# Four layer norms whose squares are taken during the product ahead of them, about a mean of four chunks, and summed on VectorE

## What is computed

```python
x_lat = layer_norm_2(DEEPNORM_ALPHA * x_lat + (1 + g1) * m_lat, ln1_g[l], ln1_b[l])      # ln1_l
f_lat = swiglu(x_lat * (1 + sc2) + sh2, w_ffn_gate[l], w_ffn_up[l], w_ffn_down[l])
x_lat = layer_norm_2(DEEPNORM_ALPHA * x_lat + (1 + g2) * f_lat, ln2_g[l], ln2_b[l])      # ln2_l

def layer_norm_2(x, g, b):
    mu = jnp.mean(xf, axis=-1, keepdims=True)
    var = jnp.mean(jnp.square(xf - mu), axis=-1, keepdims=True)
    y = (xf - mu) * lax.rsqrt(var + NORM_EPS) * g + b
```

## Time and profile before

| | |
|---|---|
| time, median of 3 runs | 2913.59 us (2911.48 to 2914.23) |
| the profiled execution: its own time, its span | 2915.59 us, 2913.8 us |
| TensorE busy (matmul) | 2683.3 us, 92% of the span |
| VectorE busy | 788.1 us, 27% |
| ScalarE busy | 457.9 us, 16% |
| mean granted TensorE clock | 0.965 |

### The profile page before, as it was taken

One profiled execution on the slowest core, in us unless ns is written; L12 is line 12 of the kernel. 1 busy time (PEld: TensorE's weight loads), 2 busy tenths in 40 slices (PEclk: granted clock), 3 DMA queues, 4 the chain that ended last, 5 costly groups with the idle time before them and its releaser, 6 DMA issues.

```text
span 2913.8 us, 33994 instructions
## 1 busy us (share of the span) xinstructions
PE 2683.3 (92%) x13754; PEld 1851.3 (64%) x13754; DVE 788.1 (27%) x1893; ACT 457.9 (16%) x973; POOL 75.2 (3%) x144
## 2 busy tenths in 40 slices
PE   6997998789998998999998799998999899999998
PEld 3555454446666773656665367687788545787887
DVE  1335113121112243111111335415542225313002
ACT  2132102231111022000000114301000123201000
POOL 0000000000000000000000000000000000000000
PEclk9998998889999999999999899999999999999999
DMA  9785998899996739999999732233675311233430
GB/s 400 323 347 213 387 376 367 329 389 409 400 420 269 276 121 387 422 412 421 420 414 422 317 133 87 87 146 134 269 288 202 116 58 63 111 145 116 154 135 15
DMA packets 117628, 764.86 MB, mean 262 GB/s; under 512 B 12832, under 2 KB 15648, under 8 KB 34272
## 3 DMA queue, kind: packets, MB, share of 16 engines
q1 hardware_dynamic: 94400, 680.57, 58.0%
q0 software_dynamic: 20224, 74.26, 6.5%
q10 hardware_dynamic: 2848, 7.83, 0.7%
HBM read 759.20 MB, written 3.41 MB: 262 GB/s over the span
## 4 chain that ended last, share of the span: by engine, by line
PE 81%; DMA 10%; DVE 5%; ACT 2%; issue 2%; SPq 1%; ACTq 0%; DVEq 0%
PE bank L570 78%; DMA ring<-in_stream 9%; PE bank L888 1%; PE bank L574 1%; PE bank L877 1%; SPq L449 1%; DVE MX L1970 1%; DVE work L1910 1%; DMA work<-in_stream 1%; DVE work L1987 0%; ACT work L1434 0%; ACT work L1504 0%; DVE X L2187 0%; DVE work L1813 0%; ACT L1434 0%
## 5 line engine op out<-in xcount | busy, mean ns | idle before, releaser
L570 PE MATMUL bank<-A,ring 128*128 128x256 f32 (+1 forms) x3088 | 711.8, 390 | 14.5 <-issue 7.2
L570 PEld LDWEIGHTS bank<-A,ring 128*128 128x128 f32 x3088 | 589.3, 192 | 132.4 <-issue 45.5
L570 PE MATMUL bank<-ring,A 128*32 128x512 f32 (+3 forms) x2304 | 389.8, 621 | 52.6 <-DMA ring<-in_stream 44.9
L570 PE MATMUL bank<-work,ring 128*128 128x256 f32 x1696 | 382.4, 382 | 5.7 <-DVE work L2445 2.1
L570 PEld LDWEIGHTS bank<-work,ring 128*128 128x128 f32 x1696 | 321.2, 190 | 56.5 <-issue 3.9
L570 PE MATMUL bank<-work 128*64 128x128 f32 (+5 forms) x2084 | 324.1, 334 | 19.1 <-DMA work<-in_stream 7.5
L570 PEld LDWEIGHTS bank<-ring,A 128*32 128x32 f32 (+2 forms) x2304 | 124.0, 127 | 300.5 <-issue 217.5
L570 PEld LDWEIGHTS bank<-work 128*128 128x128 f32 (+2 forms) x2084 | 245.4, 174 | 77.1 <-issue 45.4
L570 PE MATMUL bank<-A,work 128*128 128x256 f32 x1280 | 286.6, 381 | 0.2
L570 PEld LDWEIGHTS bank<-A,work 128*128 128x128 f32 x1280 | 240.3, 190 | 53.2 <-issue 21.1
L570 PE MATMUL bank<-ring,work 128*32 128x512 f32 (+1 forms) x1036 | 140.3, 609 | 9.2 <-DMA ring<-in_stream 8.5
(11 more groups left out here) (267 smaller groups left out, 1473.8 us busy)
## 6 DMA issues: line engine op xcount, KB each, us to landing
ring<-in_stream SPq DMA_DIRECT2D x648, 1024.0 KB, 12.5
work<-in_stream POOLq DMA_DIRECT2D x134, 512.0 KB, 9.1
X<-in_xt ACTq DMA_DIRECT2D x1, 2048.0 KB, 13.9
spill<-work ACTq DMA_DIRECT2D x3, 512.0 KB, 10.5
work<-spill POOLq DMA_DIRECT2D x3, 512.0 KB, 5.0
tab_sb<-in_tab_a ACTq DMA_DIRECT2D x1, 1120.0 KB, 18.6
X<-in_ctx2t ACTq DMA_DIRECT2D x1, 1024.0 KB, 16.4
out<-X SPq DMA_DIRECT2D x4, 256.0 KB, 2.3
```

Of the source, the lines that this page charges most:

```text
L570: return pay(pe.matmul(o, w, x, start=start, stop=stop, tile_position=place), tells)
```

## The change

Every number of chunk below is of the eight. After the product's fourth group (`SHIFT_BY` = 4), TensorE sums chunks 0 to 3 over partitions, with one matmul inside the fifth group. VectorE makes of it `SHIFT`, the mean of those 512 features per token, subtracts it from chunks 0 to 3, and sets chunks 4 to 7 to ALPHA times the old value less `SHIFT` ahead of their product; these chunks are then finished by one instruction each, straight from the bank. ScalarE squares each chunk as it comes, still in two `SQ` buffers, and VectorE adds the squares of chunks 0 to 6 in `SQSUM` and chunks 4 to 6 in `XSUM`. (As chunks 0 to 3 sum to zero after the shift over all their features, they need not be in this second sum.) TensorE sums both over partitions with two matmuls placed two matmuls ahead of the last group's end, `XSUM` into `bank[6]`, `SQSUM` into `bank[5]`. After the product only chunk 7 is left: its own value and its square, a matmul each. The three 8-column instructions that fold the gain and bias of the next product into `FG` and `FB` move from behind `center` to ahead of the last group. VectorE then makes `MEAN`, `DEV2` (mean times sum) and the variance, subtracts `MEAN` chunk by chunk, and this subtraction runs two chunks ahead of the multiplication by the reciprocal root.

```diff
+SHIFTED = ("ln1_0", "ln2_0", "ln1_1", "ln2_1")
+SHIFT_BY = 4
...
+        SHIFT, SQSUM, DEV2 = wk(12544, T), wk(13056, T), wk(16384, T)
...
+            def stats(name, j, K):
+
+                i = SHIFTED.index(name)
+
+                def at(k):
+
+                    if j == SHIFT_BY and k == K // 2:
+                        pe.wait_ge(xsum_ready, 2 * i + 2)
+                        mm(bank[6][:, 0:T], ones, XSUM, True, True, tells=True).then_inc(sum_ready, 1)
+                    if j == KD - 1 and k == K - 2:
+                        pe.wait_ge(xsum_ready, 2 * i + 3)
+                        mm(bank[6][:, 0:T], ones, XSUM, True, False)
+                        pe.wait_ge(square_added, (KD - 1) * (i + 1))
+                        mm(bank[5][:, 0:T], ones, SQSUM, True, False)
+                return at
+
+            def last_stats(name, stage):
+
+                i = SHIFTED.index(name)
+                wait_taken(pe, stage, KD - 1)
+                mm(bank[6][:, 0:T], ones, X[:, KD - 1, 0:T], False, True, tells=True).then_inc(sum_ready, 1)
+                pe.wait_ge(square_made, KD * (i + 1))
+                mm(bank[5][:, 0:T], ones, SQ[:, (KD - 1) % 2, 0:T], False, True, tells=True).then_inc(sum_ready, 1)
...
-                    linear(f"out{l}", j, w, lambda k: tile(f"l{l}_out", j * KD + k), lambda k: MG[:, k, 0:w], KD)
+                    linear(f"out{l}", j, w, lambda k: tile(f"l{l}_out", j * KD + k), lambda k: MG[:, k, 0:w], KD,
+                           wait=stats(f"ln1_{l}", j, KD))
                     if j % 4 == 3:
                         used()
-                wait_taken(pe, f"out{l}", KD - 1)
-                norm(f"ln1_{l}", w, mean=True)
+                last_stats(f"ln1_{l}", f"out{l}")
...
-                    linear(f"down{l}", j, w, lambda k: tile(st, at + k), lambda k: HB[:, k, 0:w], KF)
+                    linear(f"down{l}", j, w, lambda k: tile(st, at + k), lambda k: HB[:, k, 0:w], KF,
+                           wait=stats(f"ln2_{l}", j, KF))
...
-                wait_taken(pe, f"down{l}", KD - 1)
-                norm(f"ln2_{l}", w, mean=True)
+                last_stats(f"ln2_{l}", f"down{l}")
...
+            def stats(name, stage):
+
+                i = SHIFTED.index(name)
+                act.activation(OPEN[:, :], EPS[:, 0:1], ACT.Sqrt)
+                for k in range(KD):
+                    if k < SHIFT_BY:
+                        act.wait_ge(xc_ready, KD + (SHIFT_BY + KD) * i + k + 1)
+                    else:
+                        wait_taken(act, stage, k)
+                    if k >= 2:
+                        act.wait_ge(square_added, (KD - 1) * i + k - 1)
+                    act.activation(SQ[:, k % 2, 0:T], X[:, k, 0:T], ACT.Square).then_inc(square_made, 1)
+                act.wait_ge(var_ready, i + 1)
+                act.activation(RSTD, RSTD, ACT.Sqrt, bias=EPS[:, 1:2], scale=1.0 / D).then_inc(std_ready, 1)
...
+            def spread(name, scaled):
+
+                i = SHIFTED.index(name)
+                dve.wait_ge(sum_ready, 3 * i + 3)
+                link(dve.tensor_scalar(MEAN[:, 0:T], bank[6][:, 0:T], 1.0 / D, None, ALU.mult))
+                link(dve.tensor_tensor(DEV2, MEAN[:, 0:T], bank[6][:, 0:T], ALU.mult))
+                dve.wait_ge(sum_ready, 3 * i + 4)
+                dve.tensor_tensor(RSTD, bank[5][:, 0:T], DEV2, ALU.subtract).then_inc(var_ready, 1)
+
+                def even(k):
+
+                    dve.tensor_tensor(X[:, k, 0:T], X[:, k, 0:T], MEAN[:, 0:T], ALU.subtract).then_inc(xc_ready, 1)
+
+                even(0)
+                even(1)
                 root(name, T)
                 for k in range(KD):
-                    dve.tensor_tensor(X[:, k, 0:T], X[:, k, 0:T], RSTD[:, 0:T], ALU.mult).then_inc(mid_ready, 1)
+                    if k + 2 < KD:
+                        even(k + 2)
+                    dve.wait_ge(xc_ready, KD + (SHIFT_BY + KD) * i + SHIFT_BY + k + 1)
+                    scaled(k).then_inc(mid_ready, 1)
...
-            def outer(l, stage, gate, w, ahead=None):
-
+            added = [0]
+
+            def add_square(i, k):
+
+                dve.wait_ge(square_made, KD * i + k + 1)
+                if k > 1:
+                    dve.wait_ge(square_added, added[0])
+                m = dve.tensor_tensor(SQSUM, SQ[:, 0, 0:T] if k == 1 else SQSUM, SQ[:, k % 2, 0:T], ALU.add)
+                m.then_inc(square_added, 2 if k == 1 else 1)
+                added[0] += 2 if k == 1 else 1
+
+            def outer(l, name, stage, gate, ahead=None, fold_in=None):
+
+                i = SHIFTED.index(name)
                 for j in range(KD):
                     if ahead and j == 5:
                         ahead()
-                    b = take(stage, j)
-                    for s in range(w // T):
-                        m = dve.tensor_scalar(RT[:, j % 2, s * T:(s + 1) * T], b[:, s * T:(s + 1) * T],
-                                              MODP[:, l, gate + j, s:s + 1], None, ALU.mult)
-                    link(m)
-                    dve.scalar_tensor_tensor(X[:, j, 0:w], X[:, j, 0:w], ALPHA, RT[:, j % 2, 0:w], ALU.mult, ALU.add)\
-                       .then_inc(taken["D"], 1)
-                    if j:
+                    if j == SHIFT_BY:
+                        dve.wait_ge(sum_ready, 3 * i + 2)
+                        link(dve.tensor_scalar(SHIFT, bank[6][:, 0:T], 1.0 / (SHIFT_BY * P), None, ALU.mult))
+                        for k in range(SHIFT_BY, KD):
+                            m = dve.scalar_tensor_tensor(X[:, k, 0:T], X[:, k, 0:T], ALPHA, SHIFT, ALU.mult, ALU.subtract)
+                        link(m)
+                        for k in range(SHIFT_BY):
+                            dve.tensor_tensor(X[:, k, 0:T], X[:, k, 0:T], SHIFT, ALU.subtract).then_inc(xc_ready, 1)
+                    if j == KD - 1 and fold_in:
+                        fold(*fold_in)
+                    p, g = take(stage, j, T), MODP[:, l, gate + j, 0:1]
+                    if j < SHIFT_BY:
+                        link(dve.tensor_scalar(RT[:, j % 2, 0:T], p, g, None, ALU.mult))
+                        dve.scalar_tensor_tensor(X[:, j, 0:T], X[:, j, 0:T], ALPHA, RT[:, j % 2, 0:T], ALU.mult, ALU.add)\
+                           .then_inc(taken["D"], 1)
+                    else:
+                        dve.scalar_tensor_tensor(X[:, j, 0:T], p, g, X[:, j, 0:T], ALU.mult, ALU.add).then_inc(taken["D"], 1)
+                    if j < SHIFT_BY and j:
                         wait_taken(dve, stage, j)
-                        sum_up(j, w)
+                        m = dve.tensor_tensor(XSUM, X[:, 0, 0:T] if j == 1 else XSUM, X[:, j, 0:T], ALU.add)
+                        if j == SHIFT_BY - 1:
+                            m.then_inc(xsum_ready, 1)
+                        else:
+                            link(m)
+                    if j in (SHIFT_BY + 1, SHIFT_BY + 2):
+                        wait_taken(dve, stage, j)
+                        m = dve.tensor_tensor(XSUM, X[:, SHIFT_BY, 0:T] if j == SHIFT_BY + 1 else XSUM, X[:, j, 0:T], ALU.add)
+                        if j == KD - 2:
+                            m.then_inc(xsum_ready, 1)
+                        else:
+                            link(m)
+                    for k in {SHIFT_BY: (1, 2, 3), SHIFT_BY + 1: (4,), KD - 2: (5, 6)}.get(j, ()):
+                        add_square(i, k)
...
-                outer(l, f"out{l}", 16, w)
+                outer(l, f"ln1_{l}", f"out{l}", 16, None, (("ln1_g", l * KD, KD), ("ln1_b", l * KD, KD), l, 24, 32))
...
-                outer(l, f"down{l}", 40, w, None if l else second_mods)
+                outer(l, f"ln2_{l}", f"down{l}", 40, None if l else second_mods,
+                      None if l else (("ln2_g", 0, KD), ("ln2_b", 0, KD), 1, 0, 8))
                 if l == 0:
                     layer_norm("ln2_0", ("ln2_g", 0, KD), ("ln2_b", 0, KD), 1, 0, 8)
                 else:
-                    center("ln2_1", w)
-                    dve.wait_ge(xc_ready, NXC["ln2_1"] + KD)
-                    norm("ln2_1", w, lambda k: X[:, k, 0:w], lambda k: X[:, k, 0:w],
-                         [(0, w, lambda k: par_("ln2_g", KD + k, 1))])
+                    spread("ln2_1", lambda k: dve.scalar_tensor_tensor(X[:, k, 0:T], X[:, k, 0:T], par_("ln2_g", KD + k, 1),
+                                                                       RSTD[:, 0:T], ALU.mult, ALU.mult))
...
```

More of the change, by code:

```diff
@@ L160 @@
     NBASE[_n], NSTAT[_n], NMEAN[_n], NOUT[_n], NMID[_n], NXC[_n] = _b, _i, _m, _o, _d, _x
-    _b += NCHUNK[_n]
+    _b += 0 if _n in SHIFTED else NCHUNK[_n]
     _d += NCHUNK[_n]
-    if _n[:2] == "ln":
+    if _n == "ln_in":
         _m += 1
@@ L375, in build_program @@
         xsum_step, xsum_ready, x_done, a_again = (sem(n) for n in ("xsum_step", "xsum_ready", "x_done", "a_again"))
+        square_made, square_added, var_ready = sem("square_made"), sem("square_added"), sem("var_ready")
```

(36 more changed lines are left out.)

## The result

The changed kernel takes 2899.86 us (median of 7 runs, 2895.93 to 2906.66), the kernel before, over the 7 runs taken by then, 2919.86 (2911.48 to 2926.01). The ratio is 0.9939, 95% interval 0.9928 to 0.9950: 18 us faster, with 14.6 to 21.0 in the interval (the medians are 20.0 us apart, the means 17.5). The forecast difference was 18.8 us. The forecast time was 2894.8 with a range up to 2899.7, and the median lies just outside it. The kernel before had moved too: its first three runs, on which the forecast stood, are the lowest of its seven. One execution of the kernel before in a later set took 7049.62 us, in a slow state, and is in no comparison here.

What follows compares the result with a forecast made beforehand. TensorE bounds the kernel, with 58.5 us in four stretches behind products. Gains of 5.3, 6.1, 4.8 and 2.55 sum to 18.8 us, taking the median of 2913.59 to 2894.8, range 2890.3 to 2899.7.

Steps and rivals of the forecast that it cites:

- How the numbers follow: Closing step for the whole execution: chances of each case, range 2890.3 to 2899.7 us, faster by over 5.8 us at 0.97.
- The stretch behind the product, 6.65: From a product's last matmul to the next product's start: 6.65 us, before 13.48 at the first.
- The added matmuls, 0.432 each: Three ones matmuls for each norm inside the product at full clock: 0.432 us each, 1.30 us together.
- `out` held up for 0.15 us: In out, TensorE waits 0.15 us for the sum of the fourth chunk, so out costs 1.45 us.
- `ln1_0`, 4.8 by the strip: Behind ln1_0 VectorE is late with the first modulation strip, 0.6 us after TensorE needs it: a gain of 4.8 us.
- `ln2_0`, 5.3: Gain at ln2_0: 13.24 less 6.65 and less 1.30 for the added matmuls, 5.3 us.
- `ln1_1`, 6.1: Gain at ln1_1: 14.20 less 6.65 and less 1.45 for out's added cost, 6.1 us.
- The clock, "the same loss": At three restarts TensorE's half clock, falling after the idle stretch, costs 1.7, 1.7 and 2.7 us as before; chance 0.5.
- Rival 1: VectorE's alternating subtractions and multiplications don't overlap, 0.42 us each in place of 0.336: 3.5 us lost, 2898.3; chance 0.08.
- Rival 2: In out TensorE waits for SHIFT's sum or the last square's add, 1.4 us in each out: 2897.6; chance 0.08.
- Rival 3: Slower than before: TensorE restarts colder at half clock, even only if three restarts lose 6.3 us more each; chance 0.02.
- Rival 4: The norm's end was bound by something else, such as a strip's transfer: 2913.6 + 5.5 or no change; chance 0.02.

Runs made afterwards that it cites:

- `ln2_0` alone: Only ln2_0 and ln2_1 in the new form, ln1_0 and ln1_1 as in the kernel before: 2910.32 us, ratio 0.9976 to the kernel before.
- filler: Changed kernel plus eleven unused ones matmuls behind the last square's in ln1_0, ln2_0 and ln1_1: 2896.12 and 2898.21 us, ratios 0.9933 and 0.9931 to the kernel before.
- moved strip: Changed kernel with the idle matmuls, and behind ln1_0 the first modulation strip ahead of gain and bias on X: 2898.18 us, ratio 0.9937 to the kernel before.

## Why the prediction was right or wrong

**The range, and with it the absolute time, failed.** The step that failed is the last of "How the numbers follow": "with 1.4 on either side, half the spread of the runs shown (2911.48 to 2914.23)". The same kernel's runs in this study have medians of 2917.7 to 2919.9 and go from 2910.45 to 2927.65: half that spread is 8.6 us and not 1.4. `out0`, ahead of which nothing changed, starts anywhere in 14 us. The forecast difference of 18.8 taken from 2919.86, the kernel before's median by then, gives 2901.1, and 2899.86 is 1.2 us from that. I took the profile's 2 us over the median for a constant, when it was a hint of that scatter. Why the first three runs lay so low stays open. Only 3 of the 50 runs of the kernel before in the later sets are as low as 2914.23, so chance alone explains it poorly, and the profile taken with those three differs from the later one by 5.55 us ahead of `out0` and by 0.35 behind. On which side of 2899.7 the changed kernel falls is itself within its scatter: its second set has a median of 2897.80.

**The difference was right,** 18.8 against 19.0 and 18.9 in the profiles' changed part, and 14.6 to 21.0 by the runs. By its terms:

- *The stretch behind the product, 6.65:* measured 6.57, 6.64, 6.57. Every step of the list held to 0.1 us.
- *The added matmuls, 0.432 each:* 0.44 by doubling them. 0.67 would have been the lone one's price.
- *`out` held up for 0.15 us:* 29.30 - 27.89 = 1.41 for `out0`, of a predicted 1.45; 0.1 of it is left over the three matmuls. The cover at the group's end was 0.6 us (2006.35 to 2006.93), not 1: the last add ended when counted, 26.8 us after `out0`'s first matmul, and TensorE came for it 0.4 earlier than counted.
- *`ln1_0`, 4.8 by the strip:* the gain to the strip's sum is 4.4 us (2032.19 - 1979.52 = 52.67 against 57.04), but not by that mechanism. I had forecast that TensorE would wait 0.6 us for VectorE. VectorE's side was right: the strip ends 22.6 us behind the product (2031.46), counted were 22.7. But TensorE came after the strip, 16.80 us behind its restart in place of 15.67, because 5.7 us behind the restart were at half clock in place of 3.4. Only with that removed did the wait appear, of 0.78 us.
- *`ln2_0`, 5.3:* 5.0 with a slower start of `f1`; `ln2_0` alone 5.3. *`ln2_1`, 2.55:* 17.54 - 13.62 - 1.30 = 2.6.
- *`ln1_1`, 6.1:* 7.05. The gap gave 6.2 of it, and 0.8 came from a half clock that cost 1.9 us behind the restart and not the 2.7 that I had carried over.
- *The clock, "the same loss":* wrong at each place (1.1 more, 0.3 more, 0.8 less) and right within 0.6 in the sum, which was luck. It had the fall behind the idle stretch, as in the earlier trace rows for the first two. In the changed kernel the half clock lasted 6.8 us at each of the three places, the long form that the prediction had priced at 2898.2, but it began inside the idle stretch, and TensorE loses nothing to it while it is idle. Why it begins there is not shown. The cost itself is: filler removes it.
- *Rival 1, no overlap on VectorE:* refuted by the 0.33 to 0.34 between the alternating instructions of 0.42. The Trainium skill's exception, that an instruction which isn't held starts earlier ("VectorE: DVE Perf Modes", The DRAIN you can't avoid), agrees with these 0.33 to 0.34 us. *Rival 2:* `out` took 1.41 more and not 2.8, and VectorE's sums and squares were there when TensorE came at the group's end. *Rival 3:* the half clock cost 1.9 to 2.8 us behind a restart and not over 6. *Rival 4:* refuted, as each stretch got shorter by what was counted.

What stays open: whether the 3 to 4 us that filler and the moved strip save from `out0` on reach the whole execution. Three profiles say so; the timed runs, with intervals of 4 to 5 us on either side, don't contradict it and don't show it. And what moves the half clock from one place to another by 1 to 2 us isn't known beyond the rows above.

## What to carry to other kernels

A statistic over a product's output costs, behind the product, what can't be done before its last chunk; centring about an early estimate lets all but one chunk be squared while TensorE works, at the price of three matmuls in its stream. In these kernels a step that shortened an idle stretch of TensorE didn't give back the half clock behind it; cheap filler matmuls did, in the profile, and then the next engine's backlog shows. When a forecast is given as an absolute time, its range needs the scatter of the unchanged part, which one profile and three runs don't give; compare profiles from the first changed instruction on.

## What the runs showed that was not expected

From `out0` on, profiles of one kernel agree to 0.4 us in 915 to 937 (918.5 and 918.3; 937.5 and 937.2; 915.3 and 915.2; 924.6 and 924.5), while the 1975 us ahead of it scatter over 14. An idle stretch of TensorE that is 1.7 us longer can cost more than 1.7: behind `ln2_0` and `ln1_1` another 0.5 and 1.1 us at half clock, both times, while behind `ln1_0` it cost 0.6 less. And a half clock of the same 6.8 us costs 2.8, 2.0 and 1.9 us, by how much of it falls into the idle stretch.
